# Two attentions on one Trainium2 core: the weighing moved one unit later, high halves ahead of the exponent, and one half tile of every other unit made by GpSimd

## What is computed

```python
def block_attention(q, k, v):
    # 16 query heads, blocks of 128 queries
    s = jnp.einsum('bqhgd,bkhd->bhgqk', qi, k) * dk ** -0.5
    p = jax.nn.softmax(s, axis=-1)
    return jnp.einsum('bhgqk,bkhe->bqhge', p, v)
# layer 1 (GQA): latents attend to all 768 tokens, context tokens to the 256 of the context
# layer 2 (MLA): latents attend to all 768 tokens
```

## Time and profile before

| | us |
|---|---|
| median of 3 runs (2598.22 to 2599.84) | 2598.61 |
| the profiled execution: its own time | 2602.68 |
| the profiled execution: span of the trace | 2600.9 |
| GQA attention, first reduction to last subtraction, about | 179.1 to 363.0 |
| MLA attention, likewise | 1108.4 to 1263.9 |

### The profile page before, as it was taken

The page is one execution under the profiler, slowest core; times in us unless marked ns, Lnnn a source line. Parts: engine busy times, 40 slices in busy tenths (PEclk is TensorE's granted clock), DMA queues, the critical chain, the costliest instruction groups (busy, mean ns, idle before and its releaser), DMA issues.

```text
span 2600.9 us, 39022 instructions
## 1 busy us (share of the span) xinstructions
PE 2470.7 (95%) x16410; PEld 1439.0 (55%) x16410; DVE 1630.2 (63%) x2478; ACT 1039.5 (40%) x1666; POOL 727.5 (28%) x789
## 2 busy tenths in 40 slices
PE   6999999999999999899989999999999999999999
PEld 3566665665565585477554444735644445744444
DVE  4469964868844345888677744479966774533341
ACT  3457753433311124677444322333352234523230
POOL 0210000649999603300041000016454552011100
PEclk8999999999999999999999999999999999999999
DMA  6520014124444331300236645232212323233340
GB/s 246 180 80 18 2 50 146 52 88 146 154 154 162 138 122 47 106 18 2 61 102 201 203 163 178 79 106 69 86 57 92 111 100 118 66 95 99 99 146 33
DMA packets 224046, 271.40 MB, mean 104 GB/s; under 512 B 10047, under 2 KB 181438, under 8 KB 220798
## 3 DMA queue, kind: packets, MB, share of 16 engines
q1 hardware_dynamic: 217486, 247.05, 29.5%
q0 software_dynamic: 5280, 18.64, 2.0%
q10 hardware_dynamic: 1104, 3.21, 0.3%
HBM read 252.62 MB, written 10.49 MB: 101 GB/s over the span
## 4 chain that ended last, share of the span: by engine, by line
PE 74%; DVE 15%; ACT 6%; issue 2%; DMA 2%; POOL 1%; ACTq 0%; DVEq 0%; POOLq 0%
PE PS L326 22%; PE PS L328 21%; PE PS L327 21%; PE PS L1074 2%; DVE WB L305 2%; DVE SM L1167 2%; ACT WB L293 2%; DVE AR L1173 2%; ACT AR L1117 1%; DMA WS<-in_w_ada 1%; DVE X L1450 1%; PE PS L558 1%; DVE GT L1459 1%; DMA WS<-in_mlp_w 1%; DMA EB<-in_s_lam_im 1%
## 5 line engine op out<-in xcount | busy, mean ns | idle before, releaser
L326 PE MATMUL PS<-H,WB 128*128 128x512 bf16 (+1 forms) x1976 | 686.4, 347 | 20.8 <-DVE WB L305 8.0
L327 PE MATMUL PS<-H,WB 128*128 128x512 bf16 (+1 forms) x1976 | 685.5, 347 | 0.0
L328 PE MATMUL PS<-H,WB 128*128 128x512 bf16 (+1 forms) x1976 | 684.9, 347 | 0.0
L305 DVE TENSOR_TENSOR WB<-WS,WB 128x2048 bf16<-128x2048 f32 (+2 forms) x154 | 348.2, 2262 | 265.6 <-ACT WB L293 265.5
L293 ACT ACTIVATE WB<-WS 128x2048 bf16<-128x2048 f32 (+2 forms) x154 | 275.1, 1787 | 399.5 <-PE PS L328 222.9
L326 PE MATMUL PS<-AR,WB 128*128 128x512 bf16 (+1 forms) x1140 | 369.9, 324 | 8.9 <-DVE WB L305 8.1
L327 PE MATMUL PS<-AR,WB 128*128 128x512 bf16 (+1 forms) x1140 | 369.6, 324 | 0.0
L328 PE MATMUL PS<-AR,WB 128*128 128x512 bf16 (+1 forms) x1140 | 369.6, 324 | 0.0
L326 PEld LDWEIGHTS PS<-H,WB 128*128 128x128 bf16 x1976 | 194.9, 99 | 214.3 <-issue 22.0
L328 PEld LDWEIGHTS PS<-H,WB 128*128 128x128 bf16 x1976 | 194.9, 99 | 167.1 <-issue 3.0
L327 PEld LDWEIGHTS PS<-H,WB 128*128 128x128 bf16 x1976 | 195.0, 99 | 163.3 <-issue 5.3
(11 more groups left out here) (497 smaller groups left out, 4293.1 us busy)
## 6 DMA issues: line engine op xcount, KB each, us to landing
WS<-in_mlp_w SPq DMA_DIRECT2D x64, 1024.0 KB, 5.7
WS<-in_w_ada SPq DMA_DIRECT2D x40, 1024.0 KB, 5.1
WS<-in_w_in SPq DMA_DIRECT2D x26, 1024.0 KB, 5.1
WS<-in_ada_w SPq DMA_DIRECT2D x24, 1024.0 KB, 5.2
WS<-in_ffn_w_in SPq DMA_DIRECT2D x44, 512.0 KB, 4.9
WS<-in_ffn_w_out SPq DMA_DIRECT2D x10, 1024.0 KB, 4.9
AR<-in_w_ada SPq DMA_DIRECT2D x8, 1024.0 KB, 13.0
e_scratch<-EB POOLq DMA_DIRECT2D x16, 512.0 KB, 3.1
```

The source lines that it names most:

```text
L305: e.tensor_tensor(lo, staged_as(i, lo), hi, SUB).then_inc(dv.sem, dv.mark(("lo", i)))
L326: e.matmul(out_, l[0], r[0], start=start, stop=False)
L327: e.matmul(out_, l[0], r[1], start=False, stop=False)
L328: return e.matmul(out_, l[1], r[0], start=False, stop=stop)
```

## The change

There are four parts.

1. Order on PE: in step i `weigh` is now for unit i - 4 and stands ahead of `turn(i - 2)`; `out_turn` is for the group of unit i - 7 and stands right behind `turn`.
2. Order on ACT: `high(i - 3)`, `out_high` (i - 8), and `exponent(i - 1)` last.
3. Order on DVE: `divide` (i - 5), `low(i - 3)`, `largest(i)`, `out_low` (i - 8). `steps` grows by two.
4. POOL: for units with odd r over 768 keys (the second latent unit of each period in GQA, every other unit in MLA), ACT evicts the second part as f32 into one buffer (`Q.turned`, 384 columns), which frees the bank. POOL copies it to the bf16 high half and then subtracts for the low half. DVE does nothing for that part, and `weigh` of such a unit waits for POOL too. In MLA `attention_pool` stands in POOL's queue ahead of `residual_pool` of "w20".

```diff
             for i in range(Q.steps):
                 if i < Q.n:
                     scores(i)
+                if 0 <= i - 4 < Q.n:
+                    weigh(i - 4)
                 if 0 <= i - 2 < Q.n:
                     turn(i - 2)
-                if 0 <= i - 3 < Q.n:
-                    weigh(i - 3)
-                if whole := Q.group_at(i - 6):
+                if whole := Q.group_at(i - 7):
                     out_turn(*whole)
...
             def high(u):
                 for i in range(len(Q.order[u][0].parts)):
+                    if Q.by_pool(u, i):
+                        if u > Q.every:
+                            po.wait_ge(e, ("low", t, u - Q.every))
+                        pe.wait_ge(e, ("T", t, u, i))
+                        e.activation(Q.turned, Q.turned_at(u, i), COPY).then_inc(ac.sem, ac.mark(("turned f32", t, u), ("free", ("T", t, u, i))))
+                        continue
...
             for i in range(Q.steps):
-                if 0 <= i - 1 < Q.n:
-                    exponent(i - 1)
-                if 0 <= i - 2 < Q.n:
-                    high(i - 2)
+                if 0 <= i - 3 < Q.n:
+                    high(i - 3)
...
-                if whole := Q.group_at(i - 6):
+                if whole := Q.group_at(i - 8):
                     out_high(*whole)
+                if 0 <= i - 1 < Q.n:
+                    exponent(i - 1)
...
             for i in range(Q.steps):
-                if whole := Q.group_at(i - 4):
-                    divide(i - 4, *whole)
+                if whole := Q.group_at(i - 5):
+                    divide(i - 5, *whole)
+                if 0 <= i - 3 < Q.n:
+                    low(i - 3)
                 if i < Q.n:
                     largest(i)
-                if 0 <= i - 2 < Q.n:
-                    low(i - 2)
...
-                if whole := Q.group_at(i - 6):
+                if whole := Q.group_at(i - 8):
                     out_low(*whole)
+
+        def attention_pool(e, Q):
+            t, x = Q.tag, Q.turned
+            for u in range(Q.n):
+                if not Q.by_pool(u, 1):
+                    continue
+                hi, lo = Q.pt(u, 1)
+                ac.wait_ge(e, ("turned f32", t, u))
+                if u > 2:
+                    pe.wait_ge(e, ("W", t, u - 3))
+                e.tensor_copy(hi, x).then_inc(po.sem, po.mark(("pool high", t, u)))
+                po.wait_ge(e, ("pool high", t, u))
+                e.tensor_tensor(lo, x, hi, SUB).then_inc(po.sem, po.mark(("low", t, u)))
```

More of the change, by code:

```diff
@@ L1016, in build, with __init__, by_pool @@
         class Attention:
-            def __init__(self, tag, order, P, PT):
+            def __init__(self, tag, order, P, PT, turned, every):
                 self.tag, self.order, self.P, self.PT = tag, order, P, PT
                 self.n = len(order)
-                self.steps = self.n + 7
+                self.turned, self.every = turned.rearrange("p (k n) -> p k n", n=128), every
+                self.steps = self.n + 9
+            def by_pool(self, u, i):
+                A, r = self.order[u]
+                return r % 2 == 1 and i == 1 and len(A.parts) == 2
             def scores_at(self, u):
@@ L1083, in weigh @@
                 dv.wait_ge(e, ("low", t, u))
+                if Q.by_pool(u, 1):
+                    po.wait_ge(e, ("low", t, u))
                 for k in range(A.nk):
@@ L1216, in build @@
         CONTEXT = Pass("ctx", [4, 5], (512, 256), GOT[2:4], gqa_q, gqa_k, gqa_v(4), "O2", 696, True)
-        GQA = Attention("gqa", [unit for r in range(32) for unit in ((LATENT, 2 * r), (LATENT, 2 * r + 1), (CONTEXT, r))], GP, GPT)
+        GQA = Attention("gqa", [unit for r in range(32) for unit in ((LATENT, 2 * r), (LATENT, 2 * r + 1), (CONTEXT, r))], GP, GPT, arena(17176, 384), 3)
         OUT = columns_of(0, 8)
@@ L2120, in build @@
         LAYER2 = Pass("mla", [0, 1, 2, 3], (0, 768), MOT, mla_q, mla_k, mla_v, "O", 688, False)
-        MLA = Attention("mla", [(LAYER2, r) for r in range(64)], MP, MPT)
+        MLA = Attention("mla", [(LAYER2, r) for r in range(64)], MP, MPT, arena(23296, 384), 2)
         def mla_pe(e):
@@ L2143, in mla_pool @@
             zeros_pool(e, AR[:, 12288:20480], 256)
+            attention_pool(e, MLA)
         def wo1_pe(e):
@@ L3668, in gpsimd @@
             qkv_pool(e)
+            attention_pool(e, GQA)
             norm_pool(e, "wo0", (0, 1))
```

## The result

| | before | changed |
|---|---|---|
| median, us | 2599.23 (4 runs) | 2646.66 (2643.99 to 2647.94, 4 runs) |
| ratio on record, with 95% interval | | 1.0172 [1.016, 1.0185] |
| profiled execution, us | 2602.68 | 2643.99 |
| GQA, first start to last start of the units' transposes, us | 180.4 | 202.6 |
| MLA, likewise | 148.9 | 166.0 |

A forecast was written before the change was run, and what follows sets the result against it. It took PE, busy 95%, as the bound, waiting mostly for DVE's low halves in GQA and one group wait in MLA. 16.7 (MLA) + 29.4 (GQA) + 2 (ends) = +48 us gave 2647, range 2615 to 2668.

The forecast's parts named there:

- The wait of the group's transposes: MLA: out_turn's bank needs 1.68 us from turn's start, only 0.66 covered, so PE waits 1.02 us instead of 0.50.
- The wait for `out_low`: MLA: out_low queues behind the next unit's reduction, so that unit's second part of transposes waits a new 0.70 us.
- Four units of MLA: MLA's repeat takes 10.59 us against 9.40, +1.19 in some 14 of 16 groups: +16.7 us.
- GpSimd's chain: GQA: from the second part's transposes through ACT's eviction and POOL's copy and subtraction to weigh takes 2.94 us.
- GQA's period: GQA: 6.66 us a period against 5.68, alternating 6.95 and 6.37, over some 30 of 32 periods: +29.4 us.
- `weigh` waiting for POOL: PE's weigh of the unit POOL helps with waits 0.8 us a period in GQA and never in MLA.
- Ends: End of each attention: the last weigh comes a step later and its input through POOL, +1 us each, +2 in all.
- DVE's operations beside GpSimd: In the attentions DVE's operations have at most one wide SBUF operand, so by the skill's rule they do not contend with GpSimd.
- A: Rival: POOL is quick enough not to be waited for, only group waits stay; +24 us, 2623; chance 0.22 including everything between.
- C: Rival: DVE's relief decides, groups wait no longer; GQA falls to 4.9 us a period, -25 us, 2574; chance 0.06.
- B: Rival: POOL is slower beside DVE, copy at 1.24 us or blocked about 0.5; +16 us, 2663; chance 0.15.

The follow-up runs named there:

- run with `out_low` first: Changed kernel with one edit: in DVE's step the group's out_low stands ahead of the next unit's largest; 2623.5 us, 1.0088 against the kernel before.
- run with the own bank: Changed kernel with one edit: in MLA the group's transposes take PSUM bank 7, unused there, instead of a bank shared with the units' transposes; 2619.5 us.
- run without GpSimd: Changed kernel's order on PE, ACT and DVE, but DVE and ACT make all halves and GpSimd does nothing; 2635.3 us, 1.0129 against the kernel before.
- the old order: Order of the kernel before; with only a separate bank for MLA's group added to that kernel, 2594.0 us, 0.997 against it.
- the best one: Changed kernel with GQA's out_turn right behind scores, GpSimd on the unit's first part, and a separate bank for MLA's group; 2586.7 us, 0.9941 against the kernel before.
- run with the first part: Changed kernel with out_turn right behind scores, its halves a step sooner, and GpSimd taking its unit's first part instead of the second; 2590.3 us.

## Why the prediction was right

The forecast was 2647 and the median 2646.66. The mechanism was right, and the closeness is luck: two errors of 6 to 7 us met. The terms of the forecast add up to 48; in the traces they come to 41.3 (17.1 in MLA, 22.2 in GQA, 2.0 elsewhere), since GQA's term was 7 us too large. The medians lie 47.4 us apart, 6.1 more than the two profiled executions. By its own steps:

- **The wait of the group's transposes, 1.02 us instead of 0.50.** Held: 1.00, out of a lead of 1.69 us (forecast 1.68). The lead is 1.70 in twelve of the sixteen groups and 1.89 in the first three.
- **The wait for `out_low`, 0.70 us in MLA.** Held: 0.68. The run with `out_low` first took it away, and the run with the own bank took away both waits and 24.7 us.
- **Four units of MLA at 10.59, +16.7 us.** 10.75 and +17.1. PE's step is 2.19 instead of 2.15: six transposes take 0.69 where they took 0.66, seen also with the own bank, cause not tested.
- **GpSimd's chain of 2.94 us.** Too long: 2.75. The copy took 0.50 where 0.70 was chosen, and the subtraction 0.91 instead of 1.01; ACT's start after the transposes was 0.64 for the 0.54 that I took.
- **GQA's period of 6.66, alternating 6.37 and 6.95, +29.4 us.** The alternation is there: periods begin with the scores at 241.19, 247.38, 254.13 (above) and 260.32, so they last 6.19, 6.75 and 6.19, mean 6.47. Both kinds are 0.2 shorter than forecast, and the chain was priced 0.19 too long. That is 6 of the 7 us by which this term was too large (22.2 in the transposes' extent).
- **`weigh` waiting for POOL 0.8 us a period.** Less: 0.54 from start to start at 259.08 (0.38 printed), and 8.4 us in all by the run without GpSimd. In the MLA of the changed kernel it occurs only twice, both times at the end, as good as never.
- **Ends, +2.** Neither shown nor refuted. From one profiled execution to the other the stretch ahead of GQA's transposes grew by 2.1 us and that between the attentions by 2.5, while that behind them shrank by 2.7. In the thirteen traces the stretch between the attentions runs from 747.9 to 752.6 us and that behind them from 1337.1 to 1345.1, far more than 2 us, without a pattern by kernel.
- **The 6.1 us between the traces and the medians.** The profiled execution of the changed kernel (2643.99) lies 2.7 below its median, that of the kernel before (2602.68) 3.4 above. Where the median executions have them was not found.
- **DVE's operations beside GpSimd.** The prediction says that they have at most one wide operand in SBUF. One line does not: L321, the low half of a quarter of a weight tile, four times in each attention, has both inputs there. There the two engines did hold each other up (last section); in the changed kernel it cost about 1 us of their time.

The starts of the scores named above:

```profile
241.19 0.38 PE L1068 MATMUL PS<-AR 128*128 128x512 bf16 x1
...
247.38 0.38 PE L1068 MATMUL PS<-AR 128*128 128x512 bf16 x1
...
260.32 0.38 PE L1068 MATMUL PS<-AR 128*128 128x512 bf16 x1
```

Of the rivals, A lay nearest to the truth for GpSimd's part. C, DVE's relief deciding, fell with the first trace: DVE was idle a quarter of GQA. B's blocking did not occur with the attentions' own DVE instructions: no subtraction of POOL in the changed kernel took more than 0.93 us.

## What to carry to other kernels

A wait for a buffer has a lead, here 1.7 us from a transpose to its free bank where DVE is not behind (up to 2.2 in the GQA of the run without GpSimd). What it costs is the lead less the work that stands between in the waiting engine's queue: moving a filler of 0.52 us away added 0.50 us although no dependency changed. An instruction that frees a buffer should not stand behind one that needs work which the buffer's next user holds up: here that cost 20 us. Before helping a busy engine, look for the wait that the help does not touch: here one spare bank took 7.4 us off the old order, GpSimd's help 5.4 off the best one, and GpSimd paid only when its chain began with the part that was ready first.

## What the runs showed of the hardware

The two operations of POOL, over all 64 of each (duration in ns min/median/max, first and last start):

```profile
L1218 POOL CAST AR<-AR x64: 501/503/572, 186.7 to 1305.3; 128x384 bf16<-128x384 f32 x64
L1220 POOL TENSOR_TENSOR AR<-AR x64: 909/914/923, 187.3 to 1305.9; 128x384 bf16<-128x384 f32 x64
```

DVE was at work during all 64 of the subtractions, and they differ by 1.5% at most. For the attentions' own DVE instructions (at most one input in SBUF) the Trainium skill, "SBUF — State Buffer", section "Who interferes with whom", says that they do not contend with GpSimd, outside the modes in which DVE takes two ports; the run agrees.

L321, with two inputs in SBUF, is the exception. The first row below shows it alone, in the kernel before. The next two show it in the changed kernel, begun 0.32 us behind a subtraction of POOL. The last two are from the run with the first part, where it begins just ahead of POOL's copy.

```profile
197.21 0.68 DVE L321 TENSOR_TENSOR WB<-WS,WB 128x512 bf16<-128x512 f32 x1
```

```profile
198.29 0.91 POOL L1220 TENSOR_TENSOR AR<-AR 128x384 bf16<-128x384 f32 x1
198.61 1.13 DVE L321 TENSOR_TENSOR WB<-WS,WB 128x512 bf16<-128x512 f32 x1
```

```profile
192.53 0.68 DVE L321 TENSOR_TENSOR WB<-WS,WB 128x512 bf16<-128x512 f32 x1
192.54 1.04 POOL L1218 CAST AR<-AR 128x384 bf16<-128x384 f32 x1 [3.58 <-ACT AR L1137]
```

Whichever began first kept its usual time, and the other took up to 0.54 us longer. In the nine traces with these POOL operations (1088 of them) all sixteen that took over 5% more than usual overlap an L321 that had begun before; the longest are 1.04 us for a copy and 1.37 for a subtraction. The kernel's other DVE instructions in the attentions show nothing of the kind.

The f32 to bf16 copy of 384 columns took 0.50 us, nearer to the 0.4 estimated from "GPSIMD Engine Reference" of the Trainium skill, section "Engine selection", than to the 0.70 chosen from the earlier trace rows. The subtraction at 384 columns (0.91) does not lie on the line through 256 and 512 columns (0.87 and 1.16), which had given 1.01.
